# Late expert search spread over five half-table passes, and three-product value matmuls from the middle of the seventh pass

## The chip, the cores and the metric

The kernel runs on one core of one Trainium2 chip. The metric is the device time of one execution in microseconds, lower is better. Times are medians of three runs unless a sentence says otherwise; the profile is one further execution, and all rows come from it.

## What is computed

The reference is one decoder layer on 1024 tokens of width 1024: three gated token mixers, a residual and a LayerNorm, and then a product-key expert layer ("PEER") with a second residual and LayerNorm. The change touches only the expert layer:

```
q  = h @ w_q                                   # 8 heads x 2 halves x 128
s1, i1 = top_k(q1 . keys1, 16);  s2, i2 = top_k(q2 . keys2, 16)
cand = s1[:, None] + s2[None, :]               # 256 candidates of a head
top, pos = top_k(cand, 16);  idx = i1[pos] * 128 + i2[pos]
gate = softmax(top)
act  = gelu(h . u_tab[idx])                    # 128 experts of each token
out  = sum(gate * act * v_tab[idx])
```

`u_tab` and `v_tab` have 16384 rows of 1024 float32 numbers, 64 MB each.

## The kernel before

**Blocks and passes.** The expert layer works on 8 blocks of 128 tokens. The u rows are gathered per token: for one of the 128 slots of a block, POOL issues one indirect DMA that brings 128 rows of 4 KB (512 KB) into one of 7 places of `u_ring` (L994), and DVE multiplies them with the residual and sums (a "dot", L2400). The v rows are not gathered. The 128 token x 128 slot coefficients of a block are spread into a table of 128 x 128 keys (`table`, coefficient of expert row by token, mostly zeros), and the whole value table is streamed past it: SP loads tiles of 128 v rows (512 KB) into the 4 places of `v_ring` (L892), and PE multiplies each tile with the matching column block of `table` and adds into PSUM (`values_of`, L1391). One **pass** streams half of the value table, 64 tiles; a block needs two passes, and two blocks are in flight at a time, so there are nine passes, numbered here 0 to 8 like `p` in the code. Passes 0 and 8 have one block in flight, the others two. A float32 product of 128x512 is two instructions in the profile, so a tile of passes 1 to 6 is 8 of them, a tile of passes 0 and 8 is 4.

**What a pass holds beside the products.** In the first 28 tiles (`DOT_TILES`) of pass p DVE makes the last 56 dots of block p+1, and ACT its GELU, DVE its coefficients (L2405). At tile 30 (`TURN_TILE`) PE transposes keys and coefficients (`turn`, L1070); it waits there for DVE's coefficients. In tiles 32 to 63 the table of block p+1 is built, 4 tokens a tile: DVE makes one-hot rows (`hots`, L2392, L2393), ACT scales them (L1803), PE multiplies them (`pair`, L1377), ACT copies the result into `table` (`pair_out`, L1815). DVE makes the first 72 dots of block p+2 in the same tiles. Only two sets of one-hot buffers exist, so `hots` for one group of tokens waits for the `pair` two groups before.

**The late search.** The experts of blocks 4 to 7 are found while the passes run. Each block has four parts (two heads each); a part is four steps on DVE (`late_topk`), one a tile, and one set of small products on PE (`late_scores`, L1405). `topk_at` places them: passes 0 to 3 each run the four parts of one block in tiles 1 to 23 (a part every `SEARCH_TILES` = 6), at tile 24 the gates of that block (`late_gates`, `late_exps`), and at tile 25 ACT stores picks and gates in DRAM (`late_stored`), from where SP loads them at tile 48 of the next pass (`load_picks`). Most of the search's scratch lies in the one-hot buffers `hot1`, `hot2`, the picks `idxu` too; therefore `hots` waits for the store (`tk_out`).

**The split products.** In pass 7 alone PE runs three fp32r products in place of one float32 product (`split_values_of`, L1423; one instruction each, 12 a tile): coefficient and value are both split into a high part (fp32r) and a low part, and high x high, high x low and low x high are summed. ACT makes the high parts (`high_parts`: two copies of 128x128 from `table`, L1846, then one of the value tile, L1847); DVE subtracts for the low parts (`low_parts`: L2445 twice, then L2447) and so frees the place in `v_ring` (`low_made`, for which SP waits). In every other pass the place is freed by PE (`v_used`). There are two buffer sets: ACT may begin the set of a tile once PE has finished the tile two before (`split_used`). The value parts lie in `u_ring`, which is empty by then, the coefficient parts in `hot1_0` and `hot1_1`.

**The end of a block.** At tile 1 of pass p DVE adds block p-2 from PSUM to the residual (`add_rows`, L2413), after waiting for its last product of the pass before (`closed`); at tiles 3, 4, 7 and 8 it makes the second LayerNorm (`finish`). PE waits for `summed` before it starts the next block in the same PSUM banks.

Of the kernel before, what the change touches and what calls it, by code (L numbers as in the profile page):

```python
# [27 lines left out]
F32 = mybir.dt.float32  # L28
# [41 lines left out]
EARLY_DOTS = 72  # L70
SEARCH_TILES = 6
# [138 lines left out]
def layer(nc, A):  # L210
# [26 lines left out]
    with ctx:  # L237
# [190 lines left out]
        def raw_at(name, offset, k):  # L428
# [9 lines left out]
                    for part in range(2)] for i in range(2)]  # L438
        split_c = [nc.alloc_sbuf_tensor_at(f"split_c{i}", [P, 2, 2, P], F32R, offset=where[f"hot1_{i}"]) for i in range(2)]

        def late_topk_tiles(free):
# [16 lines left out]
            t.idxu = lay("idxu", "hot2_1", 1024, [P, SLOTS], U32)  # L458
# [86 lines left out]
        high_made, low_made, split_used = sem("high_made"), sem("low_made"), sem("split_used")  # L545
# [66 lines left out]
        def last_split(p, i):  # L612

            return NTILE * (p - NBLK + 1) + i
# [59 lines left out]
        def _(sp):  # L674
# [325 lines left out]
        def _(pe):  # L1000
# [397 lines left out]
            def late_scores(p, tb, q):  # L1398
# [3 lines left out]
                if q >= 2:  # L1402
                    pe.wait_ge(TK.sem, TK.after("rest", late_item(tb, q - 2)))
# [4 lines left out]
            def split_values_of(p, i):  # L1408

                m = last_split(p, i)  # L1410
                vhi, vlo = split_v[m % 2]
                c_of = split_c[m % 2]
                for n in in_flight(p):
                    if n == p and i == 0:
                        pe.wait_ge(summed, p - 1)
                    for a, v in ((0, vhi), (0, vlo), (1, vhi)):
                        if n == in_flight(p)[0]:
                            if a == 0 and v is vhi:
                                pe.wait_ge(high_made, m + 1)
                            elif a == 0:  # L1420
                                pe.wait_ge(low_made, m + 1)
                        for c in range(2):
                            last = pe.matmul(ps[2 * (n % 2) + c][:, :], c_of[:, n % 2, a, :], v[:, HALF * c:HALF * c + HALF],  # L1423
# [4 lines left out]
                last.then_inc(split_used, 1)  # L1428
# [7 lines left out]
            for p in range(NBLK + 1):  # L1436
                for i in range(NTILE):
# [18 lines left out]
        def _(act):  # L1456
# [379 lines left out]
            def high_parts(p, i):  # L1836

                j, m = NTILE * p + i, last_split(p, i)
# [16 lines left out]
            for p in range(NBLK + 1):  # L1855
                for i in range(NTILE):
# [4 lines left out]
                    if p == NBLK - 1:  # L1861
                        high_parts(p, i)
                    if p < NB:
                        part = topk_at(p, i)
                        if part and part[2] == 0 and part[:2] != (NB - 1, 3):
                            load_scores(4 * part[0] + part[1] + 1)
                        if i == 4 * SEARCH_TILES:
                            late_exps(p)
                        if i == 4 * SEARCH_TILES + 1:
                            late_stored(p)  # L1870
# [12 lines left out]
        def _(dve):  # L1883
# [139 lines left out]
            def late_topk(tb, q, part):  # L2023
                topk(late, late_item(tb, q), part, 4 + q % 2, late.idxu[:, 2 * TOPK * q:2 * TOPK * (q + 1)], late.gex[:, 2 * q:2 * q + 2, :],
# [351 lines left out]
            def hots(n, sub):  # L2376
# [11 lines left out]
                if sub == 1 and 1 <= n <= NB:  # L2388
                    dve.wait_ge(tk_out, late_stores(n))
# [49 lines left out]
            def low_parts(p, i):  # L2439

                j, m = NTILE * p + i, last_split(p, i)
                dve.wait_ge(high_made, m + 1)
                vhi, vlo = split_v[m % 2]
# [10 lines left out]
            for p in range(NBLK + 1):  # L2454
                for i in range(NTILE):
# [5 lines left out]
                    if p < NB and i == 4 * SEARCH_TILES:  # L2461
                        late_gates(p)
# [5 lines left out]
                    if p == NBLK - 1:  # L2468
# [33 lines left out]
```

## Time and profile before

| | before |
|---|---|
| median of three runs | 4051.45 us (4048.8 to 4055.97) |
| the profiled execution's own time | 4052.45 us |
| its span, first to last instruction | 4050.6 us |
| mean granted TensorE clock | 0.958 of full |
| busy share of the span: PE, DVE, ACT, POOL | 91%, 66%, 31%, 39% |
| bytes moved | 1133.97 MB, mean 280 GB/s |

The span is 1.85 us shorter than the execution's own time, and that execution lies 1.0 us above the median. PE, DVE, ACT and POOL are TensorE (matmul), VectorE, ScalarE and GpSimd; PEld is TensorE's weight load, SP the queue that issues the plain DMAs. The nine passes fill the last 2080 us of the span. A busy PE is not a PE at its peak: a float32 product is counted busy as long as it streams.

### The profile page before, as it was taken

The numbers are of one execution on the slowest core, as the hardware profiler recorded it, in microseconds if no ns is written. First come the engines' busy times: TensorE is split into PE (matmuls) and PEld (weight loads), VectorE is DVE, ScalarE is ACT, GpSimd is POOL, SyncE is SP. The second block draws the span as 40 slices with busy tenths as digits, with TensorE's granted clock in tenths as the row PEclk, the third lists the DMA queues.
The fourth block names the chain that finished last, engine by engine and source line by source line (L and its number), as shares of the span: only waits on it lengthen the run. The fifth ranks groups of instructions, "written<-read, shape, count | busy, mean of one in ns | idle before, by whom it ended". The sixth has DMA issues, their size and how long they took to land.

```text
span 4050.6 us, 45984 instructions
## 1 busy us (share of the span) xinstructions
PE 3694.7 (91%) x14431; PEld 2458.7 (61%) x14431; DVE 2655.6 (66%) x5440; ACT 1235.9 (31%) x2640; POOL 1577.4 (39%) x1341
## 2 busy tenths in 40 slices
PE   6999989898888979867779999898999999999998
PEld 5778768677777768656444454453544545445763
DVE  1445542248777766666999889889877868743540
ACT  1333332222333232224342240330412404224530
POOL 2556534331222157655344443444444444410000
PEclk8999999999999989988889999999999999999999
DMA  7666633346777658878999999999999999963567
GB/s 244 202 226 221 214 101 96 98 154 238 240 222 233 221 183 261 276 237 316 320 379 400 380 394 377 375 378 376 399 401 392 401 410 397 396 256 127 185 204 268
DMA packets 506327, 1133.97 MB, mean 280 GB/s; under 512 B 41180, under 2 KB 250508, under 8 KB 505904
## 3 DMA queue, kind: packets, MB, share of 16 engines
q1 hardware_dynamic: 335120, 570.94, 40.5%
q0 software_dynamic: 147456, 536.94, 35.4%
q10 hardware_dynamic: 23584, 24.12, 1.7%
q8 instruction: 73, 1.20, 0.1%
q14 instruction: 94, 0.77, 0.1%
HBM read 1044.81 MB, written 89.41 MB: 280 GB/s over the span
## 4 chain that ended last, share of the span: by engine, by line
PE 34%; DVE 14%; DMA 3%; issue 2%; ACT 1%; DVEq 0%; ACTq 0%
PE ps L1391 27%; DVE u_ring L2400 5%; PE ps L1377 4%; PE ps L1423 2%; DMA u_ring<-in_peer_u,pidx 2%; DVE split_v L2447 1%; DMA v_ring<-in_peer_v 1%; ACT split_v L1847 1%; DVE hot L2392 1%; DVE hot L2393 1%; DVE inds_own L1961 0%; DVE got_own L2006 0%; DVE inds_own L1949 0%; DVE left_own L1952 0%; ACT split_c L1846 0%
## 5 line engine op out<-in xcount | busy, mean ns | idle before, releaser
L1391 PE MATMUL ps<-v_ring,table 128*128 128x512 f32 x3584 | 1593.0, 595 | 17.4 <-DMA v_ring<-in_peer_v 17.2
L994 POOL DMA_INDIRECT u_ring<-in_peer_u,pidx x800 | 775.1, 969 | 935.6 <-DVE coefe L2400 881.6
L1391 PEld LDWEIGHTS ps<-v_ring,table 128*128 128x128 f32 x3584 | 663.9, 191 | 772.9 <-issue 725.1
L2400 DVE CUSTOM_DVE_ANT_0 u_ring<-u_ring,h_up 128x1024 f32<-128x1024 f32 x800 | 948.2, 1217 | 137.4 <-DMA u_ring<-in_peer_u,pidx 126.5
L1053 PE MATMUL ps<-x_hi,w_hi 128*128 128x512 f32 x1280 | 516.8, 404 | 39.2 <-ACT w_hi L1499 23.6
L1056 PE MATMUL ps<-x_lo,w_hi 128*128 128x512 f32 x1280 | 506.7, 396 | 0.0
L1377 PEld LDWEIGHTS ps<-hot,hot 128*128 128x128 f32 x2048 | 282.2, 203 | 157.0 <-issue 111.1
L938 POOL TENSOR_TENSOR w_lo<-w_raw,w_hi 128x1024 fp32r<-128x1024 f32 x120 | 300.7, 2511 | 197.0 <-ACT w_hi L1499 192.2
L1815 ACT ACTIVATE table<-ps 128x512 f32<-128x512 f32 (+3 forms) x256 | 229.3, 896 | 435.8 <-PE ps L1377 435.8
L1803 ACT ACTIVATE hot<-hot,by_slot 128x128 f32<-128x128 f32 x1024 | 321.2, 388 | 75.7 <-DVE hot L2392 71.0
L959 POOL DMA_INDIRECT e_ring<-in_peer_u,icole x224 | 229.8, 1026 | 274.1 <-DVE dotse L2058 196.2
L1377 PE MATMUL ps<-hot,hot 128*128 128x128 f32 x2048 | 292.1, 289 | 36.7 <-DVE hot L2393 13.7
L1062 PE MATMUL ps<-x_hi,w_lo 128*128 128x512 f32 x1280 | 317.4, 390 | 0.3 <-POOL w_lo L938 0.2
L1053 PEld LDWEIGHTS ps<-x_hi,w_hi 128*128 128x128 f32 x1280 | 246.0, 192 | 94.2 <-issue 13.3
L2392 DVE TENSOR_TENSOR hot<-keys,by_slot 128x512 f32<-128x512 f32 x256 | 177.1, 692 | 183.8 <-PE ps L1377 173.2
L1056 PEld LDWEIGHTS ps<-x_lo,w_hi 128*128 128x128 f32 x1280 | 245.9, 192 | 52.2 <-issue 1.9
L1062 PEld LDWEIGHTS ps<-x_hi,w_lo 128*128 128x128 f32 x1280 | 239.7, 188 | 52.5 <-POOL w_lo L938 2.6
L2058 DVE CUSTOM_DVE_ANT_0 e_ring<-e_ring,h_up 128x1024 f32<-128x1024 f32 x128 | 155.0, 1220 | 127.9 <-DMA e_ring<-in_peer_u,icole 125.0
L946 POOL TENSOR_TENSOR w_hi<-w_raw,zero 128x1024 fp32r<-128x1024 f32 x56 | 110.4, 1972 | 245.1 <-PE ps L1053 112.7
L1423 PE MATMUL ps<-split_v,split_c 128*128 128x512 f32 x768 | 185.6, 397 | 3.6 <-DVE split_v L2447 1.4
L2393 DVE TENSOR_TENSOR hot<-keys,by_slot 128x512 f32<-128x512 f32 x256 | 175.7, 686 | 0.0
L1423 PEld LDWEIGHTS ps<-split_v,split_c 128*128 128x128 f32 x768 | 140.1, 188 | 48.9 <-DVE split_v L2447 18.5
(326 smaller groups left out, 4184.7 us busy)
## 6 DMA issues: line engine op xcount, KB each, us to landing
v_ring<-in_peer_v SPq DMA_DIRECT2D x576, 512.0 KB, 6.8
w_raw<-in_w_in SPq DMA_DIRECT2D x88, 512.0 KB, 5.0
wh_d<-w_hi SPq DMA_DIRECT2D x56, 512.0 KB, 2.6
wl_d<-w_lo SPq DMA_DIRECT2D x56, 512.0 KB, 4.0
w_hi<-wh_d SPq DMA_DIRECT2D x56, 512.0 KB, 4.5
w_lo<-wl_d SPq DMA_DIRECT2D x56, 512.0 KB, 4.7
u_ring<-in_peer_u,pidx POOLq DMA_INDIRECT x800, 9.2
raw_mid<-in_w_branch SPq DMA_DIRECT2D x48, 256.0 KB, 3.3
```

What stands on the lines that cost most here:

```text
L938: pool.tensor_tensor(out=w_lo[b][:, 0:k, :], in0=raw[:, 0:k, :], in1=w_hi[b][:, 0:k, :].bitcast(F32), op=ALU.subtract).then_inc(w_split[b], 1)
L959: pool.indirect_dma_start(out=e_ring[:, s, :], out_offset=None, in_=u_tab, in_offset=bass.IndirectOffsetOnAxis(ap=icole[:, r, s:s + 1], ax ...
L994: pool.indirect_dma_start(out=u_ring[:, slot_of(n, k), :], out_offset=None, in_=u_tab, in_offset=bass.IndirectOffsetOnAxis(ap=pidx[n % 2][ ...
L1053: first = pe.matmul(out, w_hi[b][:, k, :], hi[:, k, :], start=(k == 0), stop=False)
L1056: pe.matmul(out, w_hi[b][:, k, :], lo[:, k, :], start=False, stop=False)
L1062: last = pe.matmul(out, w_lo[b][:, k, :], hi[:, k, :], start=False, stop=(k == k_n - 1))
L1377: last = pe.matmul(build_bank(item)[:, P * m:P * m + P], hot2[sub % 2][:, m, :], hot1[sub % 2][:, m, :], start=True, stop=True)
L1391: last = pe.matmul(ps[2 * (n % 2) + c][:, :], table[:, row_of(n, i1), :], v_ring[:, j % V_TILES, HALF * c:HALF * c + HALF], start=(n == p ...
L1423: last = pe.matmul(ps[2 * (n % 2) + c][:, :], c_of[:, n % 2, a, :], v[:, HALF * c:HALF * c + HALF], start=(n == p and i == 0 and a == 0 an ...
L1803: last = act.activation(hot1[sub % 2][:, m, :], hot1[sub % 2][:, m, :], ACT.Copy, scale=by_slot[:, 2, t0 + m:t0 + m + 1])
L1815: last = act.activation(table[:, r0:r0 + near, t0:t0 + TOK].rearrange("p i t -> p t i"), src[:, :, 0:near], ACT.Copy)
L2400: dve.tensor_tensor_reduce(out=u_ring[:, slot_of(n, k), :], in0=u_ring[:, slot_of(n, k), :], in1=h1_up[:, :, :].rearrange("p c n -> p (c n)"),
```

## The change

Three things are changed, all in the expert layer.

- **Search.** Passes 0 to 3 run three parts each and pass 4 runs four; part number 3p + slot is counted through, so that a block's four parts lie in two passes. Gates and store follow the fourth part of a block by one and two tiles: pass 1 tiles 6 and 7, pass 2 tiles 12 and 13, pass 3 tiles 18 and 19, pass 4 tiles 24 and 25. The picks get a place of their own (`pidx_one`), and `hots` no longer waits for the store.
- **Split products** run from tile 32 of pass 6 to the end of pass 8, in place of pass 7 alone.
- **Three buffer sets** in place of two, the coefficient parts in `score_in` and the last row of `u_ring`. In passes 6 and 7 the high parts of the coefficients move from ACT to DVE, one copy of both blocks (128x256) in place of two; in pass 8 ACT makes the one copy. The low parts of both blocks are one subtraction in place of two. In pass 8, too, `v_ring` is freed by DVE's `low_made` and no longer by PE.

```diff
+SPLITS = 3
...
+        split_c = [nc.alloc_sbuf_tensor_at(f"split_c{i}", [P, 2, 2, P], F32R, offset=o)
+                   for i, o in enumerate((where["score_in"], where["score_in"] + 2 * D, where["u_ring"] + 2 * SPLITS * D * 4))]
...
-            t.idxu = lay("idxu", "hot2_1", 1024, [P, SLOTS], U32)
+            t.idxu = lay("idxu", "pidx_one", 0, [P, SLOTS], U32)
...
+        FIRST_SPLIT = NTILE * (NBLK - 2) + HALF_T
+        def split_at(p, i):
+            return NTILE * p + i - FIRST_SPLIT
+        def rows_at(p, i):
+            rows = sorted(row_of(n, tile_key(p, i)) for n in in_flight(p))
+            return table[:, rows[0]:rows[-1] + 1:max(rows[-1] - rows[0], 1), :]
+        def high_rows(p, i):
+            return (c_last, i + 1) if p == NBLK else (c_made, split_at(p, i) + 1)
...
+        def searched(p):
+            return 3 if p < NB else 4 if p == NB else 0
         def topk_at(p, i):
-            q, step = i // SEARCH_TILES, i % SEARCH_TILES - 2
-            return (p, q, step) if p < NB and q < 4 and -1 <= step < 4 else None
+            slot, step = i // SEARCH_TILES, i % SEARCH_TILES - 2
+            part = 3 * p + slot
+            return (part // 4, part % 4, step) if 0 <= slot < searched(p) and -1 <= step < 4 else None
...
-                old = j - V_TILES - NTILE * (NBLK - 1)
-                if old in range(NTILE):
+                old = j - V_TILES - FIRST_SPLIT
+                if old >= 0:
                     sp.wait_ge(low_made, old + 1)
                 else:
-                    sp.wait_ge(v_used, j + 1 - (NTILE if old >= NTILE else 0))
+                    sp.wait_ge(v_used, j + 1)
...
             def split_values_of(p, i):
...
                             if a == 0 and v is vhi:
+                                pe.wait_ge(*high_rows(p, i))
                                 pe.wait_ge(high_made, m + 1)
...
-                        if p < NB:
-                            pe.wait_ge(TK.sem, TK.after("rest", late_item(p, 3)))
+                        if searched(p):
+                            pe.wait_ge(TK.sem, TK.after("rest", late_item(0, 0) + 3 * p + searched(p) - 1))
...
-                    if p != NBLK - 1:
+                    if split_at(p, i) < 0:
                         values_of(p, i)
                     else:
                         split_values_of(p, i)
...
             def high_parts(p, i):
...
                     act.wait_ge(u_dots, dots_before(NBLK, 0) + U_ROWS)
-                    act.wait_ge(build_out, pair_item(NBLK - 1, NSUB - 1) + 1)
-                if m >= 2:
-                    act.wait_ge(split_used, m - 1)
-                for n in in_flight(p):
-                    act.activation(split_c[m % 2][:, n % 2, 0, :], table[:, row_of(n, tile_key(p, i)), :], ACT.Copy)
-                act.activation(split_v[m % 2][0][:, :], v_ring[:, j % V_TILES, :], ACT.Copy).then_inc(high_made, 1)
+                if m >= SPLITS:
+                    act.wait_ge(split_used, m - SPLITS + 1)
+                if p == NBLK:
+                    act.activation(split_c[m % SPLITS][:, 0:1, 0, :], rows_at(p, i), ACT.Copy).then_inc(c_last, 1)
+                act.activation(split_v[m % SPLITS][0][:, :], v_ring[:, j % V_TILES, :], ACT.Copy).then_inc(high_made, 1)
...
-                if sub == 1 and 1 <= n <= NB:
-                    dve.wait_ge(tk_out, late_stores(n))
...
             def low_parts(p, i):
...
+                if p == NBLK - 1 and i == 0:
+                    dve.wait_ge(build_out, pair_item(NBLK - 1, NSUB - 1) + 1)
+                if p < NBLK:
+                    if m >= SPLITS:
+                        dve.wait_ge(split_used, m - SPLITS + 1)
+                    dve.tensor_copy(c_of[:, :, 0, :], rows_at(p, i)).then_inc(c_made, 1)
                 dve.wait_ge(high_made, m + 1)
-                vhi, vlo = split_v[m % 2]
-                for n in in_flight(p):
-                    dve.tensor_tensor(out=split_c[m % 2][:, n % 2, 1, :], in0=table[:, row_of(n, tile_key(p, i)), :],
-                                      in1=split_c[m % 2][:, n % 2, 0, :].bitcast(F32), op=ALU.subtract)
-                last = dve.tensor_tensor(out=vlo[:, :], in0=v_ring[:, j % V_TILES, :], in1=vhi[:, :].bitcast(F32), op=ALU.subtract)
-                last.then_inc(low_made, 1)
+                dve.wait_ge(*high_rows(p, i))
+                dve.tensor_tensor(out=c_of[:, :, 1, :], in0=rows_at(p, i), in1=c_of[:, :, 0, :].bitcast(F32), op=ALU.subtract)
+                dve.tensor_tensor(out=vlo[:, :], in0=v_ring[:, j % V_TILES, :], in1=vhi[:, :].bitcast(F32), op=ALU.subtract).then_inc(low_made, 1)
...
-                    if p == NBLK - 1:
+                    if split_at(p, i) >= 0:
                         low_parts(p, i)
```

## Rows read from the trace of the kernel before

**Rows 1.** The chain of work that ended last, shares by line (page, part 4).
```profile
PE ps L1391 27%; DVE u_ring L2400 5%; PE ps L1377 4%; PE ps L1423 2%; DMA u_ring<-in_peer_u,pidx 2%; DVE split_v L2447 1%; DMA v_ring<-in_peer_v 1%; ACT split_v L1847 1%; DVE hot L2392 1%; DVE hot L2393 1%; DVE inds_own L1961 0%; DVE got_own L2006 0%; DVE inds_own L1949 0%; DVE left_own L1952 0%; ACT split_c L1846 0%
```

**Rows 2.** Busy time by stretch: halves of passes 0, 3, 4, 6; passes 7 and 8.
```profile
core 0: us, PE busy (x) PEld busy (x) DVE busy (x) ACT busy (x) POOL busy (x), PEclk, DMA share, GB/s
1963.00:2060.00 97.00, 65.82 (x170) 28.34 (x169) 90.23 (x300) 4.95 (x9) 31.19 (x33) 0.89 0.97 357
2060.00:2164.00 104.00, 90.01 (x382) 52.72 (x381) 92.87 (x159) 70.40 (x156) 51.08 (x49) 0.97 1.03 409
...
2701.00:2836.00 135.00, 118.63 (x300) 54.60 (x299) 124.38 (x360) 7.71 (x15) 56.58 (x58) 0.94 0.96 362
...
2974.00:3093.00 119.00, 114.48 (x270) 51.06 (x269) 78.58 (x133) 4.84 (x12) 56.11 (x58) 0.99 1.00 394
...
3600.00:3737.00 137.00, 137.00 (x506) 76.26 (x506) 38.81 (x60) 66.36 (x156) 0.00 (x0) 1.00 0.38 127
3737.00:3926.00 189.00, 185.45 (x770) 140.10 (x769) 110.19 (x203) 93.58 (x192) 0.00 (x0) 1.00 0.57 185
3926.00:4042.00 116.00, 112.67 (x258) 47.46 (x256) 4.61 (x9) 0.20 (x1) 0.00 (x0) 1.00 0.82 283
```

**Rows 3.** Waits at `turn` in passes 0, 1, 2, 3, 4; last, DVE's in pass 4.
```profile
PE ps L1070 <- DVE coefe L2405: 15.3, 1, 15.3
...
PE ps L1070 <- DVE coefe L2405: 3.1, 1, 3.1
...
PE ps L1070 <- DVE coefe L2405: 16.7, 1, 16.7
...
PE ps L1070 <- DVE coefe L2405: 16.4, 1, 16.4
...
PE ps L1070 <- issue: 4.5, 1, 4.5
...
DVE u_ring L2400 <- DMA u_ring<-in_peer_u,pidx: 36.9, 44, 1.4
```

**Rows 4.** Timeline of one tile, second half of pass 6: PE, then ACT, then DVE.
```profile
start us, us, engine line op out<-in xcount [idle before <-releaser]
3659.82 1.05 PE L1377 MATMUL ps<-hot,hot 128*128 128x128 f32 x8
3660.72 3.60 PE L1391 MATMUL ps<-v_ring,table 128*128 128x512 f32 x8
3664.15 1.05 PE L1377 MATMUL ps<-hot,hot 128*128 128x128 f32 x8
...
3660.92 1.07 ACT L1815 ACTIVATE table<-ps 128x512 f32<-128x512 f32 x1 [2.23 <-PE ps L1377]
3661.76 1.25 ACT L1803 ACTIVATE hot<-hot,by_slot 128x128 f32<-128x128 f32 x4
...
3660.92 0.69 DVE L2392 TENSOR_TENSOR hot<-keys,by_slot 128x512 f32<-128x512 f32 x1 [3.03 <-PE ps L1377]
```

**Rows 5.** Timeline of pass 7: ACT, then DVE.
```profile
3800.70 0.51 ACT L1846 ACTIVATE split_c<-table 128x128 fp32r<-128x128 f32 x2 [1.65 <-PE ps L1423]
3801.12 1.04 ACT L1847 ACTIVATE split_v<-v_ring 128x1024 fp32r<-128x1024 f32 x1
3803.44 0.51 ACT L1846 ACTIVATE split_c<-table 128x128 fp32r<-128x128 f32 x2 [1.28 <-PE ps L1423]
...
3806.58 0.51 ACT L1846 ACTIVATE split_c<-table 128x128 fp32r<-128x128 f32 x2 [1.68 <-PE ps L1423]
...
3802.20 0.49 DVE L2445 TENSOR_TENSOR split_c<-table,split_c 128x128 fp32r<-128x128 f32 x2 [1.49 <-ACT split_v L1847]
3802.61 1.22 DVE L2447 TENSOR_TENSOR split_v<-v_ring,split_v 128x1024 fp32r<-128x1024 f32 x1
```

**Rows 6.** The split products by line (min/median/max ns), and PEld's wait for DVE in pass 7.
```profile
L1423 PE MATMUL ps<-split_v,split_c x768: 387/389/793, 3737.3 to 3926.0; 128*128 128x512 f32 x192
...
PEld ps L1423 <- DVE split_v L2447: 18.5, 41, 1.0
```

**Rows 7.** DMA issues of pass 7 and of pass 8: count, KB, median us to landing.
```profile
v_ring<-in_peer_v SPq DMA_DIRECT2D x61, 512.0 KB, 3.4
...
v_ring<-in_peer_v SPq DMA_DIRECT2D x59, 512.0 KB, 4.6
```

More of the change, by code:

```diff
@@ L437, in layer @@
         split_v = [[nc.alloc_sbuf_tensor_at(f"split_v{part}_{i}", [P, D], F32R, offset=where["u_ring"] + (2 * i + part) * D * 4)
-                    for part in range(2)] for i in range(2)]
-        split_c = [nc.alloc_sbuf_tensor_at(f"split_c{i}", [P, 2, 2, P], F32R, offset=where[f"hot1_{i}"]) for i in range(2)]
+                    for part in range(2)] for i in range(SPLITS)]
+        split_c = [nc.alloc_sbuf_tensor_at(f"split_c{i}", [P, 2, 2, P], F32R, offset=o)
+                   for i, o in enumerate((where["score_in"], where["score_in"] + 2 * D, where["u_ring"] + 2 * SPLITS * D * 4))]
+        assert 2 * SPLITS < U_ROWS
         def late_topk_tiles(free):
@@ L634, in dots_by, with gates_at, stores_at @@
             return min(SLOTS, done)
+        def searched(p):
+            return 3 if p < NB else 4 if p == NB else 0
         def topk_at(p, i):
-            q, step = i // SEARCH_TILES, i % SEARCH_TILES - 2
-            return (p, q, step) if p < NB and q < 4 and -1 <= step < 4 else None
+            slot, step = i // SEARCH_TILES, i % SEARCH_TILES - 2
+            part = 3 * p + slot
+            return (part // 4, part % 4, step) if 0 <= slot < searched(p) and -1 <= step < 4 else None
+        def gates_at(p, i):
+            part = topk_at(p, i - 1)
+            return part[0] if part and part[1:] == (3, 3) else None
+        def stores_at(p, i):
+            return gates_at(p, i - 1)
         def head_item(h, c):
@@ L1401, in late_scores @@
                 pe.wait_ge(build_out, pair_item(p, NSUB - 1) + 1)
-                if q >= 2:
-                    pe.wait_ge(TK.sem, TK.after("rest", late_item(tb, q - 2)))
+                if 4 * tb + q >= 3 * p + 2:
+                    pe.wait_ge(TK.sem, TK.after("rest", late_item(tb, q) - 2))
                 for n in range(4):
@@ L1408, in split_values_of @@
             def split_values_of(p, i):
-                m = last_split(p, i)
-                vhi, vlo = split_v[m % 2]
-                c_of = split_c[m % 2]
+                m = split_at(p, i)
+                vhi, vlo = split_v[m % SPLITS]
+                c_of = split_c[m % SPLITS]
                 for n in in_flight(p):
@@ L1422, in split_values_of @@
                         for c in range(2):
-                            last = pe.matmul(ps[2 * (n % 2) + c][:, :], c_of[:, n % 2, a, :], v[:, HALF * c:HALF * c + HALF],
+                            last = pe.matmul(ps[2 * (n % 2) + c][:, :], c_of[:, part_of(n, p, i), a, :], v[:, HALF * c:HALF * c + HALF],
                                              start=(n == p and i == 0 and a == 0 and v is vhi),
@@ L1427, in split_values_of @@
                         last.then_inc(closed, 1)
-                last.then_inc(split_used, 1)
+                if p < NBLK or i < NTILE - 1:
+                    last.then_inc(split_used, 1)
             turn(0)
@@ L1836, in high_parts @@
             def high_parts(p, i):
-                j, m = NTILE * p + i, last_split(p, i)
+                j, m = NTILE * p + i, split_at(p, i)
                 act.wait_ge(v_in[j % V_TILES], 16 * (j // V_TILES) + 16)
@@ L1860, in _ @@
                         root(p - 2)
-                    if p == NBLK - 1:
+                    if split_at(p, i) >= 0:
                         high_parts(p, i)
[L1863 to L1870, printed above, removed]
+                    part = topk_at(p, i)
+                    if part and part[2] == 0 and part[:2] != (NB - 1, 3):
+                        load_scores(4 * part[0] + part[1] + 1)
+                    if gates_at(p, i) is not None:
+                        late_exps(gates_at(p, i))
+                    if stores_at(p, i) is not None:
+                        late_stored(stores_at(p, i))
                     if i == DOT_TILES and p + 1 < NBLK:
@@ L2023, in late_topk @@
             def late_topk(tb, q, part):
+                if tb == 0 and q == 0 and part == 0:
+                    dve.wait_ge(e_out, 32)
                 topk(late, late_item(tb, q), part, 4 + q % 2, late.idxu[:, 2 * TOPK * q:2 * TOPK * (q + 1)], late.gex[:, 2 * q:2 * q + 2, :],
@@ L2460, in _ @@
                         late_topk(*part)
-                    if p < NB and i == 4 * SEARCH_TILES:
-                        late_gates(p)
+                    if gates_at(p, i) is not None:
+                        late_gates(gates_at(p, i))
                     if p >= 2:
@@ L2467, in _ @@
                             finish(p - 2, (3, 4, 7, 8).index(i))
-                    if p == NBLK - 1:
+                    if split_at(p, i) >= 0:
                         low_parts(p, i)
```

11 lines of the change are left out of this document (6 added, 5 removed).

## The prediction

> **What bounds the kernel now.** I read the chain of waits first. Its largest share in the expert layer is PE's value products, then DVE's dots, then the table builds [rows 1]: the end is set by PE, except where DVE makes it wait. The stretches of the passes [rows 2] then show three regimes. In the second half of pass 6 PE is busy 137 of 137 us and DMA moves 127 GB/s: pure PE. In the first half of pass 3 DVE is busy 124.4 of 135 us, in that of pass 4, which has no search, 78.6 of 119 us. In the second half of pass 0 the DMA share is 1.03 at 409 GB/s. The waits say the same from PE's side: at `turn` it waits 15.3, 3.1, 16.7 and 16.4 us in passes 0 to 3 and 4.5 us in pass 4 [rows 3]. Pass 1 hardly waits because more dots of block 2 are made ahead. In pass 4 DVE itself waits 36.9 us for gathered rows [rows 3], so with the search gone the gathers are the next limit. The time-line of a tile gives the prices at the end: a pair build takes 3660.72 - 3659.82 = 0.90 us and a float32 tile 3664.15 - 3660.72 = 3.43 us, 4.33 together [rows 4].
>
> **Search, passes 0 to 3.** One part costs DVE (124.4 - 78.6) / 4 = 11.5 us [rows 2]. In passes 2 and 3 it comes off the wait of 16.7 and 16.4 us, down to some 5 us, which is also what DMA leaves (4.5 in pass 4). PE loses one set of score products too: the two half-passes differ by 16 us, the waits by 11.9 [rows 2, 3], so four sets and the slower clock after a long wait (0.94 against 0.99 [rows 2]) are worth 4 us, one set and most of the clock about 1. I take 12 us for each of these passes. Pass 1 has no wait to lose: 1 us. In pass 0 the part would take 11.5 off 15.3 us, but its first half already moves 357 GB/s with a DMA share of 0.97, and 97 us at 357 GB/s squeezed to the 409 GB/s of the next half is 85 us: at most 12, at least nothing if it is DMA that holds it. I take 10, nearer to the upper end, since DVE, not DMA, is what PE waits for there. Sum: 10 + 1 + 12 + 12 = 35 us gained.
>
> **Search, pass 4.** Four parts on a pass that had none. Its first half becomes that of pass 3 before, 135 for 119 us [rows 2]: 16 us lost. Net of the search: **-19 us**. The gates, the exponentials and the store move to earlier tiles with one answer: ACT is busy under 8 us of these halves [rows 2], and the picks are due at tile 48. The score loads of ACT's queue are as many as before. Dropping the `tk_out` wait in `hots` is worth nothing: two groups of one-hots are made under 7 us of PE work.
>
> **A split tile.** In pass 7 ACT starts a set when PE ends a tile, at 3800.70, 3803.44 and 3806.58: tiles of 2.74 and 3.14 us in turn [rows 5]. The short one is the tile without a wait, 12 products of 0.228 us; every second tile pays 0.4 us because the set comes late: two copies and the value copy 0.42 + 1.04 on ACT, 0.41 + 1.22 on DVE [rows 5], 3.1 us after a tile two before has ended, against 2.74 us. PEld's waits for DVE, 18.5 us in 41 cases [rows 6], are this.
>
> **Second half of pass 6.** 32 tiles go from 4.33 to 2.74 + 0.90 = 3.64 us: 32 x 0.69 = 22 us, less 1 for the first set: **-21 us**. That holds if ACT and DVE make a tile in 3.64. ACT: value copy 1.04, pair copy 0.84 to the next start, four scalings 1.25 [rows 4, 5] = 3.1. DVE: two one-hots of 0.69, the copy of 256 coefficients, their subtraction at 0.49, the value subtraction 1.22. The copy has no row; ACT's two copies are 0.51 and DVE's own two subtractions 0.49, one instruction of 128 numbers is half of that, so 0.25 to 0.51; I take 0.4. Sum 3.5. Both fit, closely; with three sets their hand-overs are off PE's path. What they lose as cover is PE's long float32 tile. POOL has nothing there.
>
> **Pass 7.** Three sets take the wait out: 64 x 2.74 = 175.4, and 1.1 us for the first tiles, where DVE first waits for the table's last copy and then for the last product before `add_rows`: 176.5 for 189 [rows 2]: **-12.5 us**. It can't gain more than that unless a product gets faster than 0.228 us.
>
> **Pass 8.** PE's tile goes from 4 instructions in about 1.72 us (half of 3.43) to 6 x 0.228 = 1.37 us, 88 us for 64. But a place of `v_ring` is now held by ACT and DVE: coefficient copy 0.21, value copy 1.04, subtraction 0.2, value subtraction 1.22 [rows 5], with hand-overs 2.8 us from landing to release. With four places a tile takes (landing time + 2.8) / 4. Landing takes 3.4 us in pass 7 at 185 GB/s and 4.6 us in pass 8 at 283 GB/s [rows 2, 7]: 1.55 us or 1.85 us a tile. I take 1.85, the row of the same rate of loads. That is 118 us; `finish` of block 6 sits between DVE's subtractions and shifts the ring by 3 us. 121 for 116: **+5 us**, bounds -17 and +20 (landing 5.6, if loads delay each other more). The Trainium skill, in "DMA: Bandwidth & Descriptors" under the anatomy of one DMA, puts a transfer at a fixed 2.0 us plus its bytes over 436 GB/s, for 512 KB 3.2 us as an estimate; the lone loads of pass 7 agree (3.4), those of pass 8 don't, and by it a tile would take 1.5 us and the pass about 96 us, which is rival 2.
>
> **The sum.** -19 - 21 - 12.5 + 5 = -47.5 on the profiled execution's 4052.45 us: 4005. It stood 1.0 above the median of the runs; I say **4004 us**.
>
> **Rivals.**
> 1. *The gathers hold the early passes.* The part taken away was hidden: DVE waits for rows in its place, as in pass 4 (36.9 us), and passes 0, 2 and 3 gain a third, 11 of 34 us, while pass 4 still pays. For it: DMA shares of 0.97 to 1.03 [rows 2]. Against: DVE waits on rows only where it has no search. 4004 + 23 = 4027. Chance 0.15.
> 2. *Pass 8 runs at the lone landing time*, 1.55 us a tile: 64 x 1.55 = 99 us for 116, 22 better than forecast: 3982. For it: the ring sends loads farther apart than PE did. Against: DMA's share is 0.82 at 283 GB/s [rows 2], so at 1.55 us (338 GB/s) little is left. Chance 0.14.
> 3. *PE's clock falls in pass 8.* PE would work 1.37 of 1.85 us. The granted clock was 0.89 in the first half of pass 0, where PE was busy 66 of 97 us [rows 2], and a split product then took up to 793 for 389 ns [rows 6]. At half clock all through, a tile takes 2.74 us, 175 us, +54: 4058, no change. Against: pass 0 lost it around one long wait. "TensorE: Matmul & The Clock Gate" in the Trainium skill says that an engine left idle is throttled and activity releases it. Chance 0.05.
> 4. *Slower: ACT and DVE run in lockstep in pass 6.* High parts, low parts, one-hots and scalings each wait for the other engine, with only two one-hot sets. If nothing overlaps, a tile takes 3.1 + 3.5 = 6.6 us: 32 x (6.6 - 4.33) = +73 in place of -21: 4098. It decides from about 5.4 us a tile on (32 x (5.4 - 3.64) = 56 takes up the gain and 8 us more). Against: before, the same one-hot loop left DVE idle 3.03 us a tile [rows 4], and both engines can run a tile ahead. Chance 0.03.
>
> **How the numbers follow.** The forecast has 0.55; the rest, 0.08, are mixtures of its terms' ends, mostly pass 8 slower (landing 5.6: 4019). A measurement of this kernel tells about 0.2%, 8 us, from no change. Forecast, rivals 1 and 2 and nearly all mixtures are faster: 0.93; rival 3, 0.04 same, with 0.01 of it reaching faster by a clock lost only in part; rival 4, 0.03 slower. The range takes in rivals 1 and 2 almost wholly: 3983 to 4027. The forecast alone has 3994 to 4015 (early passes +-7, pass 8 +-8).
>
> **What would show it.** At `turn` waits near 5 us in passes 0, 2, 3 and 16 in pass 4; tiles of 3.64 us in the second half of pass 6, no wait for DVE there; pass 7 about 176 us; in pass 8 PE waiting for `split_v`, loads landing in 4 to 4.6 us, the pass near 120 us. The forecast is wrong if `turn` still waits over 8 us in passes 2 and 3, if pass 6 has PE waiting for ACT or DVE in every tile, or if pass 8 is under 105 or over 135 us.

## The result and the profile after

| | before | after |
|---|---|---|
| median of 12 runs each | 4053.14 us | 4026.95 us |
| lowest and highest | 4042.63, 4060.24 | 4016.5, 4039.03 |
| ratio of the two, 95% interval | | 0.9935 (0.9923 to 0.9946) |
| the profiled execution's own time | 4052.45 us | 4033.38 us |
| from the first product of pass 0 to the last of pass 8 | 2078.9 us | 2048.5 us |

The change makes the kernel 26 us faster, a little over half of the 47 us that were forecast (4004), and the time lies at the upper end of the range of 3983 to 4027. The profiled execution after lies 6.4 us above its median, and its passes start 11 us later than those before (at 1974 for 1963 us), in code that the change doesn't touch. So the two traces are compared by the length of the passes, 30.4 us shorter, and not by their ends.

Busy time of each engine in the halves of the passes after, cut at the first value product of each half (columns as in [rows 2]):

```profile
core 0: us, PE busy (x) PEld busy (x) DVE busy (x) ACT busy (x) POOL busy (x), PEclk, DMA share, GB/s
1974.00:2063.00 89.00, 67.01 (x159) 27.53 (x158) 77.18 (x241) 2.08 (x6) 30.28 (x32) 0.94 0.97 368
...
2426.00:2558.00 132.00, 116.89 (x292) 53.51 (x291) 112.95 (x304) 7.71 (x15) 56.24 (x58) 0.95 0.97 368
...
2696.00:2828.00 132.00, 117.68 (x296) 54.05 (x295) 112.94 (x304) 7.72 (x15) 56.46 (x59) 0.95 0.97 370
...
2966.00:3100.00 134.00, 118.05 (x299) 54.40 (x298) 123.65 (x360) 7.72 (x15) 56.77 (x59) 0.94 0.96 362
...
3611.00:3726.00 115.00, 115.00 (x633) 99.64 (x632) 92.61 (x153) 97.44 (x184) 0.00 (x0) 1.00 0.48 156
3726.00:3901.00 175.00, 174.55 (x769) 143.81 (x768) 124.52 (x203) 69.80 (x69) 0.00 (x0) 1.00 0.62 200
3901.00:4022.00 121.00, 100.54 (x385) 67.47 (x384) 91.97 (x134) 77.97 (x125) 0.00 (x0) 1.00 0.80 267
```

Set beside [rows 2], the last three rows are the split products as forecast: 115 for 137 us, 175 for 189, 121 for 116. The fourth row is pass 4 with its four parts, a copy of pass 3 before. The surprise is the third: pass 3 lost a part, DVE is busy 113 us for 124, yet the half-pass takes 132 us for 135. By the start of each half-pass in the two traces the terms are:

| stretch | before | after | difference | forecast |
|---|---|---|---|---|
| pass 0 | 200.8 | 192.8 | -8.0 | -10 |
| pass 1 | 264.4 | 259.2 | -5.1 | -1 |
| pass 2, first half | 135.4 | 132.6 | -2.9 | -12 |
| pass 3, first half | 135.3 | 131.9 | -3.4 | -12 |
| pass 4, first half | 119.2 | 135.0 | +15.8 | +16 |
| pass 6, first half | 114.1 | 117.1 | +3.1 | 0 |
| pass 6, second half | 137.2 | 115.3 | -21.9 | -21 |
| pass 7 | 189.0 | 175.1 | -13.8 | -12.5 |
| pass 8 | 115.7 | 121.2 | +5.6 | +5 |

The second halves of passes 2 to 5 and pass 5 itself are as they were within 0.3 us. The 3.1 us of pass 6 belong to a longer wait at `turn` (4.2 for 2.8 us) and a dip of the clock after it; it shows in other kernels below too.

Each row of the table is one trace against one trace, and the early passes differ between executions. Over the traces of this and the next section, with the search placed as before and as after the change, pass 0 takes 196.9 to 200.8 us with four parts and 189.5 to 192.8 with three, pass 1 259.8 to 264.4 and 256.8 to 259.4, the first half of pass 2 135.2 to 135.7 and 132.6 to 134.1. The signs hold; the 5.1 us of pass 1 are at the upper end, from middle to middle they are 3.

The waits at `turn` in passes 0, 2, 3 and 4 after, then DVE's wait for gathered rows in pass 3 (what waited, for what, us in total, times, longest):

```profile
PE ps L1099 <- DVE coefe L2434: 4.5, 1, 4.5
...
PE ps L1099 <- DVE coefe L2434: 15.1, 1, 15.1
...
PE ps L1099 <- issue: 14.3, 1, 14.3
...
PE ps L1099 <- issue: 15.9, 1, 15.9
...
DVE u_ring L2429 <- DMA u_ring<-in_peer_u,pidx: 6.9, 9, 1.3
```

In pass 0 the wait fell as forecast, from 15.3 to 4.5 us, but it is not the measure of the gain there: experiments 7 and 8, with the same search, wait 10.9 and 11.1 us at `turn` in a first half that is shorter still (86.4 and 87.0 us for 89.7). PE waits for `v_ring` loads in this half too, 15.3 us after the change and 9.6 and 10.0 in those two. In passes 2 and 3 the wait at `turn` is hardly shorter than before (16.7 and 16.4 in [rows 3]), and a wait of DVE for rows, of which these half-passes had 0.7 us in pass 2 and none in pass 3, stands in the place of the search.

A tile of the second half of pass 6 after, first DVE:

```profile
3660.55 1.22 DVE L2482 TENSOR_TENSOR split_v<-v_ring,split_v 128x1024 fp32r<-128x1024 f32 x1
3661.84 0.69 DVE L2421 TENSOR_TENSOR hot<-keys,by_slot 128x512 f32<-128x512 f32 x1
3662.45 0.68 DVE L2422 TENSOR_TENSOR hot<-keys,by_slot 128x512 f32<-128x512 f32 x1
3663.05 0.28 DVE L2478 CAST split_c<-table 128x256 fp32r<-128x256 f32 x1
3663.85 0.43 DVE L2481 TENSOR_TENSOR split_c<-table,split_c 128x256 fp32r<-128x256 f32 x1 [0.51 <-ACT split_v L1877]
3664.19 1.22 DVE L2482 TENSOR_TENSOR split_v<-v_ring,split_v 128x1024 fp32r<-128x1024 f32 x1
```

The same tile on ACT:

```profile
3661.84 1.12 ACT L1846 ACTIVATE table<-ps 128x512 f32<-128x512 f32 x1 [0.51 <-PE ps L1406]
3662.74 1.07 ACT L1877 ACTIVATE split_v<-v_ring 128x1024 fp32r<-128x1024 f32 x1
3663.72 1.26 ACT L1834 ACTIVATE hot<-hot,by_slot 128x128 f32<-128x128 f32 x4
3665.47 1.13 ACT L1846 ACTIVATE table<-ps 128x512 f32<-128x512 f32 x1 [0.49 <-PE ps L1406]
```

ACT's copies into `table` are 3665.47 - 3661.84 = 3.63 us apart and it idles 0.5 us in each tile, DVE too. PE has no wait there in the trace, so it sets the pace, at the forecast 3.64 us a tile. The coefficient copy on DVE, which had no row before, takes 0.28 us, the low end of its bounds.

### The profile page after: what moved, and what is told of

The parts are those of the page before. It is cut to its first block, busy times and chain, and to the rows that moved or that the text cites. A ratio compares the mean times of both kernels' runs of the same rounds, so it can differ in the third digit from the quotient of the medians.

```text
span 4031.1 us, 47164 instructions
## 1 busy us (share of the span) xinstructions
PE 3658.6 (91%) x14687; PEld 2513.0 (62%) x14687; DVE 2809.6 (70%) x5664; ACT 1322.2 (33%) x2671; POOL 1577.5 (39%) x1341
## 4 chain that ended last, share of the span: by engine, by line
PE 33%; DVE 11%; DMA 6%; issue 2%; ACT 1%; POOL 0%; DVEq 0%; ACTq 0%
PE ps L1420 21%; PE ps L1453 6%; DVE u_ring L2429 5%; PE ps L1406 4%; DMA u_ring<-in_peer_u,pidx 4%; DMA v_ring<-in_peer_v 2%; DVE hot L2421 1%; DVE hot L2422 1%; DVE split_v L2482 1%; DMA score_in<-subkeys_t 0%; DVE got_own L2035 0%; PE h_up L1395 0%; DVE inds_own L1990 0%; DVE inds_own L1978 0%; ACT split_v L1877 0%
## 5 line engine op out<-in xcount | busy, mean ns | idle before, releaser
L1420 PE MATMUL ps<-v_ring,table 128*128 128x512 f32 x3072 | 1367.4, 596 | 19.4 <-DMA v_ring<-in_peer_v 19.2
L1420 PEld LDWEIGHTS ps<-v_ring,table 128*128 128x128 f32 x3072 | 570.1, 192 | 667.8 <-issue 632.4
L1453 PE MATMUL ps<-split_v,split_c 128*128 128x512 f32 x1536 | 370.7, 395 | 20.9 <-DVE split_v L2482 18.8
L1453 PEld LDWEIGHTS ps<-split_v,split_c 128*128 128x128 f32 x1536 | 281.3, 188 | 97.6 <-DVE split_v L2482 35.2
L2421 DVE TENSOR_TENSOR hot<-keys,by_slot 128x512 f32<-128x512 f32 x256 | 176.8, 691 | 96.2 <-PE ps L1406 71.4
L1877 ACT ACTIVATE split_v<-v_ring 128x1024 fp32r<-128x1024 f32 x160 | 168.7, 1057 | 98.1 <-PE ps L1453 98.1
```

Source lines behind the costliest of these rows:

```text
L1420: last = pe.matmul(ps[2 * (n % 2) + c][:, :], table[:, row_of(n, i1), :], v_ring[:, j % V_TILES, HALF * c:HALF * c + HALF], start=(n == p ...
L1453: last = pe.matmul(ps[2 * (n % 2) + c][:, :], c_of[:, part_of(n, p, i), a, :], v[:, HALF * c:HALF * c + HALF], start=(n == p and i == 0 an ...
```

## The experiments

Each time is the median of 4 to 10 runs; the ratio behind it, with its 95% interval, is to the kernel before, run beside it. The lengths of passes come from one profiled execution each.

Two theories stood after the result. **A:** the split products gave all of the gain and the search nothing, because the gathers have no slack: while the parts run DVE is full, the seven places of `u_ring` stay full and the gathers stop; what they miss is not made up. **B:** the bytes of a half-pass bound it, and where the search lies doesn't matter; or the search was worth its forecast and the split fell short.

**1. The split alone.** The search goes back to four parts in passes 0 to 3.

```diff
-            return 3 if p < NB else 4 if p == NB else 0
+            return 4 if p < NB else 0
...
-            part = 3 * p + slot
+            part = 4 * p + slot
```

> The change with the search put back: four parts in each of passes 0 to 3, none in pass 4; the split products and three buffer sets stay. Theory (the moved search gives nothing net; the split products give all of the gain, 21.9 + 13.8 - 5.6 = 30 us by the two traces): 30 us under the kernel before, about 4023 us, with passes 0 to 5 as long as before, the second half of pass 6 at 115 us, pass 7 at 175, pass 8 at 121. Rival (the search was worth its forecast 19 us, and it is the split that fell short): only 7 us under the kernel before.

4026.13 us, 0.9935 (0.9915 to 0.9954) of before: the same as the whole change. The median is 26.5 us under the kernel before where 30 were expected; the passes of the trace are 32.6 us shorter, 7 of them in passes 0 and 1 (197.6 and 260.5 us), whose search is that of before. Its first halves of passes 2 to 4 are 135.2, 135.2 and 118.3 us, as before; pass 6's second half 115.2, pass 7 175.1, pass 8 123.6.

**2. The search alone**, in the kernel before: the parts placed 3, 3, 3, 3, 4, pass 7 alone split, with two sets (the diff is the change's own, without its split parts).

> The kernel before with the search alone moved (3, 3, 3, 3, 4 parts); pass 7 alone is split, with two sets. Theory: within 4 us of the kernel before; the first halves of passes 0 to 3 are shorter by 8, 5, 3 and 3 us, that of pass 4 longer by 16. Rival (the forecast): 19 us faster.

4053.8 us, 1.0002 (0.9993 to 1.0012). The first halves of passes 0 to 4 take 88.7, 117.7, 133.8, 131.9 and 134.7 us: the same pattern as after the whole change. The two runs together settle it: the gain is the split's, and the moved search cancels itself.

**3. and 4. The same parts, placed differently.** In the first the steps of a part lie two tiles apart; in the second the parts follow each other without a free tile. The first `PLACES` below is that of the spread version, the second that of the clumped one.

```diff
-            slot, step = i // SEARCH_TILES, i % SEARCH_TILES - 2
+            per, steps_at = PLACES[searched(p)] if searched(p) else (64, {})
+            slot, step = i // per, steps_at.get(i % per, -2)
...
+PLACES = {3: (9, {1: -1, 2: 0, 4: 1, 6: 2, 8: 3}), 4: (7, {1: -1, 2: 0, 3: 1, 5: 2, 6: 3})}
+PLACES = {3: (5, {0: -1, 1: 0, 2: 1, 3: 2, 4: 3}), 4: (6, {1: -1, 2: 0, 3: 1, 4: 2, 5: 3})}
```

> The change with the same three parts a pass, but their steps two tiles apart over tiles 1 to 26 in place of one tile apart in tiles 1 to 17 (and the four of pass 4 over tiles 1 to 27). Nothing is computed otherwise. Theory (while parts run DVE is full and the gathers stop, because the seven places of u_ring are full; after the last part the dots left over come at the gathers' rate): DVE work of 110 us a first half is then even, the dots never fall behind the gathers, PE's wait at the turn in passes 2 and 3 falls from 15 to 5 or 6 us, each first half from 132 to about 123 us; pass 4 stays at 135 because four parts fill DVE all along; some 20 us under the change, 4007. Rival (the bytes of a first half bound it, DMA share 0.97): placement changes nothing, waits stay at 14 to 15 us, 4027.

> The other direction: the three parts of passes 0 to 3 without a free tile between them, in tiles 0 to 14; pass 4 as in the change. Theory: more dots are left when the parts end (26 for 20 of 58), the wait at the turn in passes 2 and 3 grows from 15 to about 19 us, 10 us over the change in all, 4037. Rival (bytes bound it): no difference.

Spread: 4022.64 us, 0.9923 (0.9901 to 0.9945), first halves of passes 2 and 3 129.6 and 130.9 us, waits 12.6 and 12.7 us. Clumped: 4042.29 us, 0.9977 (0.9965 to 0.9989), 136.4 and 137.9 us, 15 us over the change by the medians where 10 were expected. Its waits at `turn` did not grow to 19 us (14.7 and 14.9): PE itself gets there later, since it waits 3 us near the start, where `add_rows` comes late. Placement matters, so B's bytes alone don't bound it, but spreading brought 1 to 3 us a half-pass where 9 were expected, and by the medians it can't be told from the change. The gathers issued by POOL show why. Windows of 80, 26 and 14 us (20 in the last kernel, the third left out in two of them) from the start of a pass; the columns are POOL's busy time with the number of gathers, the granted TensorE clock, the DMA share and GB/s. First pass 3 after the change:

```profile
2696.00:2776.00 80.00, 30.49 (x31) 1.00 0.98 367
2776.00:2802.00 26.00, 13.58 (x14) 1.00 1.03 412
2802.00:2816.00 14.00, 7.62 (x9) 0.66 1.02 407
```

Pass 3 before, with four parts:

```profile
2701.00:2781.00 80.00, 30.14 (x31) 1.00 0.98 365
2781.00:2807.00 26.00, 11.01 (x12) 1.00 1.03 409
```

Pass 4 before, without a search:

```profile
2974.00:3054.00 80.00, 39.95 (x41) 1.00 1.01 400
3054.00:3080.00 26.00, 11.47 (x13) 1.00 1.03 410
```

Pass 3 with the parts spread:

```profile
2681.00:2761.00 80.00, 37.17 (x38) 1.00 1.00 384
2761.00:2787.00 26.00, 7.51 (x8) 1.00 1.03 409
2787.00:2801.00 14.00, 7.51 (x8) 0.65 1.02 394
```

Pass 3 with the parts clumped:

```profile
2692.00:2772.00 80.00, 28.46 (x29) 0.96 0.91 330
2772.00:2798.00 26.00, 12.17 (x13) 1.00 1.02 405
2798.00:2818.00 20.00, 10.61 (x12) 0.68 1.03 410
```

PE could reach `turn` about 106 us into a pass. By then pass 4 before has issued 54 gathers, pass 3 before 43, the change 45, the spread version 46, the clumped one 42 (a gather on the border of two windows counts in both). In its first 80 us pass 3 after the change runs the same three parts at the same places as before and has the same 31 gathers; leaving out the fourth part gives two gathers more. The rest must come while PE stands (the clock of 0.65 to 0.68 is read over that wait), at 394 to 410 GB/s and some 1.6 us a gather. After the parts DVE waits for rows, so no DVE time can buy the deficit back. The spread version is better early (38 for 31 in 80 us), but its last part runs from 78 to 112 us into the pass, when the change has run its last by 82 us. In pass 3 before, DVE began its coefficients 122.5 us into the pass; the four parts, gates included, kept it busy 12.7 us a part. Three parts leave 122.5 - 12.7 = 110 us of work for 106 us. That is full however they lie. After the change the coefficients began at 119.6 us, some 10 us later than this sum, and DVE stood 9.6 us before its dots that it had not stood before (6.9 for rows, 2.7 with no releaser named). Theory A holds, with its capacity put right: three parts are one too many. A `u_ring` with more places, which would test the gathers' deficit directly, was not run.

**5. Two parts in the late passes.** If so, two parts fit into the 37 us that DVE waits in a pass without search. The rest of the edit is that of 3.

```diff
+PARTS = (4, 4, 4, 2, 2)
+PLACES = {4: (6, {1: -1, 2: 0, 3: 1, 4: 2, 5: 3}), 2: (13, {1: -1, 3: 0, 6: 1, 9: 2, 12: 3})}
```

> The change with the sixteen parts placed 4, 4, 4, 2, 2 on passes 0 to 4; the two parts of passes 3 and 4 have their steps three tiles apart. Theory (from passes 2 and 4 the gathers run at their rate of about 4.8 rows in 10 us and have no slack; DVE work costs nothing while DVE still waits for rows, and costs its full time once DVE is full and the seven places of u_ring stay full): two parts, 25 us, fit into the 37 us that DVE waits for rows, so the first halves of passes 3 and 4 take 119 to 122 us, those of passes 0 to 2 what they took before (97, 122, 135); sum of the five first halves 594 us for 607 of the change, 12 us under the change, 4015. Rival (each part costs a pass about the same, 4 us): 127 us in passes 3 and 4, sum 609, no gain over the change, 4027.

4016.39 us, 0.9905 (0.9887 to 0.9923), by its median 11 us under the change. The first halves of passes 3 and 4 take 122.8 and 121.0 us. The gathers of pass 3, in the same windows:

```profile
2705.00:2785.00 80.00, 38.06 (x39) 1.00 1.02 400
2785.00:2811.00 26.00, 11.40 (x13) 1.00 1.03 410
```

And DVE's wait for rows in it:

```profile
DVE u_ring L2431 <- DMA u_ring<-in_peer_u,pidx: 15.2, 17, 1.5
```

52 gathers by 106 us for 45: two parts come almost free (DVE's wait for rows falls from 36.9 to 15.2 us), and the price of a part is not a constant: against the 119.2 us of pass 4 before, which had none, two parts cost 2 to 4 us a half-pass, three cost 10 to 13 (spread or not), four 16.

**6. Pass 8 in float32.** The split products stop at the end of pass 7.

```diff
-            return NTILE * p + i - FIRST_SPLIT
+            return NTILE * p + i - FIRST_SPLIT if p < NBLK else -1
...
-                if old >= 0:
+                if 0 <= old < NSPLIT:
                     sp.wait_ge(low_made, old + 1)
                 else:
-                    sp.wait_ge(v_used, j + 1)
+                    sp.wait_ge(v_used, j + 1 - (NSPLIT if old >= 0 else 0))
```

> The change with pass 8 alone put back to float32 products, its places in v_ring freed by PE. Theory (the ring of four places bounds pass 8: landing time plus 2.8 us of holding, over four): pass 8 goes back from 121 to 116 us, 5 us under the change, 4022. Rival (pass 8 would be as long with float32 because something else, the loads themselves or the later start of its tiles, sets it): 121 us, no difference.

4014.73 us, 0.9901 (0.9883 to 0.9919). Pass 8 takes 113.6 us for 121.2, PE busy 112:

```profile
3891.00:4005.00 114.00, 112.08 (x260) 48.09 (x258) 4.87 (x9) 0.20 (x1) 0.00 (x0) 1.00 0.83 285
```

So splitting pass 8 costs 7.6 us by the two traces; the medians are 12 apart, with intervals of some 7 us. Over all traces pass 8 takes 113.3 to 115.7 us in the five kernels that have it in float32, and 121.2 to 123.9 in the six that have it split as in the change. Experiment 1's trace shows the ring at work, first the DMA issues of its pass 8 (count, KB, median us to landing):

```profile
v_ring<-in_peer_v SPq DMA_DIRECT2D x59, 512.0 KB, 4.8
```

One tile of that pass on ACT:

```profile
3925.70 0.31 ACT L1876 ACTIVATE split_c<-table 128x128 fp32r<-128x128 f32 x1 [1.07 <-DMA v_ring<-in_peer_v]
3925.92 1.04 ACT L1877 ACTIVATE split_v<-v_ring 128x1024 fp32r<-128x1024 f32 x1
```

And on DVE:

```profile
3927.00 0.29 DVE L2481 TENSOR_TENSOR split_c<-table,split_c 128x128 fp32r<-128x128 f32 x1 [0.75 <-ACT split_v L1877]
3927.20 1.22 DVE L2482 TENSOR_TENSOR split_v<-v_ring,split_v 128x1024 fp32r<-128x1024 f32 x1
```

From ACT's start at 3925.70 to DVE's end at 3928.42 a place is held 2.72 us; with 4.8 us to land, (4.8 + 2.7) / 4 = 1.88 us a tile, and the pass is 123.6 / 64 = 1.93 in that trace and 1.89 after the change. A `v_ring` with more places, which would test the ring directly, was not run. The Trainium skill's fixed time plus bytes for one transfer ("DMA: Bandwidth & Descriptors", anatomy of one DMA; 3.2 us as an estimate) is a fit for transfers that GpSimd issues, and these loads are SP's. It is near the 3.4 us of the lone loads of pass 7 [rows 7]; once loads overlap (4.6 to 4.8 us), the trace does not agree.

**7. Two buffer sets.** `SPLITS = 2`, with the list of places for `split_c` cut to two; nothing else.

> The change with two buffer sets in place of three. Theory (the third set takes out the wait for the low parts): pass 7 back to 187 to 189 us for 175, tiles of 2.74 and 3.1 us in turn; the second half of pass 6, where the pair build of 0.9 us covers the hand-over, within 4 us of 115; pass 8 within 5 us of 121; 13 to 18 us over the change, 4042. Rival (moving the coefficient copies from ACT to DVE took the wait out, not the third set): pass 7 stays near 176 us.

4038.03 us, 0.9966 (0.9951 to 0.9981). The passes from the second half of pass 6 on:

```profile
3592.00:3708.00 116.00, 116.00 (x640) 100.40 (x638) 90.50 (x153) 99.95 (x184) 0.00 (x0) 1.00 0.47 155
3708.00:3885.00 177.00, 176.24 (x767) 143.27 (x767) 122.94 (x201) 69.29 (x67) 0.00 (x0) 1.00 0.60 195
3885.00:4020.00 135.00, 107.04 (x386) 64.98 (x384) 94.81 (x137) 79.41 (x127) 0.00 (x0) 1.00 0.76 243
```

Here the theory falls. Pass 7 takes 177.5 us, hardly more than with three sets, so the third set is not needed to take its waits out. In pass 8, where little was expected, the third set is worth 134.5 - 121.2 = 13 us (11 by the medians): its tiles mostly alternate between 1.66 and 2.40 us with two. Why they do was not followed up.

**8. Three sets, copies back on ACT.**

```diff
-                if p == NBLK:
-                    act.activation(split_c[m % SPLITS][:, 0:1, 0, :], rows_at(p, i), ACT.Copy).then_inc(c_last, 1)
+                for k, n in enumerate(sorted(in_flight(p), key=lambda n: row_of(n, tile_key(p, i)))):
+                    last = act.activation(split_c[m % SPLITS][:, k, 0, :], table[:, row_of(n, tile_key(p, i)), :], ACT.Copy)
+                last.then_inc(c_last, 1)
```

> The change with the coefficients' high parts back on ACT as two copies of 128x128, three sets kept. It tells what took the wait out of pass 7: two sets with the copies on DVE gave 177.5 us, two sets with the copies on ACT (the kernel before) 189, three sets with the copies on DVE 175. Theory (either of the two is enough, since each alone shortens the wait for a set below the 2.72 us of the products): pass 7 at 175 to 178 us, the second half of pass 6 at 115 to 118 (ACT then has 3.6 us of work a tile of 3.63), within 4 us of the change. Rival (only taking the copies off ACT helps): pass 7 at 186 us or more.

4022.38 us, 0.9933 (0.9916 to 0.9949), pass 7 at 175.5, the second half of pass 6 at 115.5 us. With the kernel before (two sets, copies on ACT: 189) the four cases are complete: either step alone takes the wait out (177.5 and 175.5 us), and both together (175.1) add 0.4 to 2.4 us. One thing is not told apart: these three kernels also make the low parts of both blocks in one subtraction, the kernel before in two. By the rows (0.43 us for 0.49, and 0.34 us for 0.41 to the next start) that is worth 0.07 us of the 3.1 that a set took, an estimate; no run has that step alone.

**9. A shorter hold in pass 8.** ACT copies the coefficients before it waits for the value tile, DVE subtracts them before it waits for the high value part.

```diff
-                act.wait_ge(v_in[j % V_TILES], 16 * (j // V_TILES) + 16)
+                if p < NBLK:
+                    act.wait_ge(v_in[j % V_TILES], 16 * (j // V_TILES) + 16)
...
                     act.activation(split_c[m % SPLITS][:, 0:1, 0, :], rows_at(p, i), ACT.Copy).then_inc(c_last, 1)
+                    act.wait_ge(v_in[j % V_TILES], 16 * (j // V_TILES) + 16)
```

> The change with pass 8's coefficient parts made before the value tile has landed: ACT copies them before it waits for the tile, DVE subtracts them before it waits for the high value part. Theory (ring): a place is held 0.4 us less, a tile takes 0.1 us less, pass 8 about 115 us for 121, 6 us under the change, 4021. Rival (DVE or the loads' rate bounds pass 8): at most 1 us.

4020.34 us, 0.991 (0.9887 to 0.9933), by the medians not clear of the change. Pass 8 takes 119.1 us, 2.1 less than after the change and not 6; it lies below all six split traces above, by 2.1 to 4.8 us. The time-lines of SP, ACT and DVE give both terms of the ring, as means over pass 8. From ACT's first use of a place to its release: 2.81 us after the change, 2.41 here, the 0.4 us that were meant. From the issue of a load to that first use: 4.83 and 5.15 us, 0.3 more. The ring holds as a sum, (5.15 + 2.41) / 4 = 1.89 us a tile, but its two terms are not independent. Part of the 0.3 us is in the loads: in tiles where ACT stood waiting for its load the time from the issue is 4.74 and 5.00 us. That the loads queue on each other because they are issued closer together is argued, not shown.

**10. and 11. Put together.** The first takes 5 and 6. The second places the parts 3, 4, 4, 3, 2, the threes spread.

> The change with both gains of the single experiments: the parts placed 4, 4, 4, 2, 2 and pass 8 in float32 products. Theory (they are in different passes and add): 12 + 7.5 us under the change, 4007 us. Rival (one took what the other gave, or the single ones were noise): 4015, as either alone.

> As the run before, but the parts placed 3, 4, 4, 3, 2, those of passes with three parts spread two tiles apart. Theory: the first half of pass 0 at 86 to 90 us for 95 to 97, that of pass 3 at 130 for 123, the rest the same; within 3 us of the run before, 4006. Rival (a lead won in pass 0 is lost in pass 1, which waits for the same gathers): 5 us slower than the run before.

4006.46 us, 0.9895 (0.9878 to 0.9911), and 4003.26 us, 0.9883 (0.9866 to 0.9899). The two gains add. Either version beats both kernels, by 20 to 24 us the change and by 45 to 48 the kernel before; the two can't be told apart (pass 0's first half is 84.2 us for 98.0, pass 3's 130.2 for 122.9). In the first one the sum of the passes is 2022.0 us for 2048.5 after the change, in the second 2026.9. The lead that pass 0 wins is not lost in pass 1 (259.7 and 259.8 us), against the last rival.

## Why the prediction was right and wrong

The direction and the three terms of the end were right, each within 2 us by the trace: **pass 6** -21.9 for -21, **pass 7** -13.8 for -12.5, **pass 8** +5.6 for +5. **Pass 4** (+15.8 for +16) was right because pass 3 before was its exact model. **Pass 0** gave 8 of 10.

The step that failed is "In passes 2 and 3 it comes off the wait of 16.7 and 16.4 us, down to some 5 us". The wait stayed at 15.1 and 14.3 us, over the 8 that the prediction itself named as the sign of being wrong, and the half-passes gave 2.9 and 3.4 us in place of 12 each, 17.7 us short. The search as a whole came to -3.6 us for -19, since pass 1 gave 4 us more than forecast. The 11.5 us of DVE time did go (busy 124.4 to 112.9 us). The step in effect took the time to the coefficients for the larger of two times, DVE's 110 us of work and the 107 us at which the gathers let pass 4 have them without a search. But the two share a buffer of seven rows: in a time when DVE is full the gathers lose what they can't catch up, since once DVE frees places DMA already moves 394 to 412 GB/s. So the times partly add. The rows for it stood in the prediction, DVE's 36.9 us of waiting for rows in pass 4 above all, and rival 1 named the mechanism, with a third of the gain left (4027). In passes 2 and 3 it was this rival that came true, at 3 of 12 us. What was argued against it, that DVE waits on rows only where it has no search, is true of the first halves before (to within 2 us) only because there DVE was the longer of the two. That the median, 4026.95 us, falls on rival 1's figure is partly luck: rival 1 gave passes 0, 2 and 3 together 11 us and they took 14, pass 1 took 4 more than forecast, pass 6 lost 3 in its first half, and the two traces differ by 30.4 us where the medians differ by 26.2.

Pass 1 was missed the other way, -5.1 for -1 (some -3 over all traces): its wait at `turn` of 3.1 us, taken as a floor, vanished, and so did a set of score products.

In pass 7 the size was right and the cause half right. "Three sets take the wait out" was one of two sufficient causes; experiments 7 and 8 show that moving the copies does it as well. In pass 8 the ring of four places gave the right time, 1.85 us a tile and 3 us for `finish` (1.89 measured over the pass, both together). That the third set matters most there, 13 us, the prediction did not see.

Rival 2 (lone landing times) fell: loads took 4.8 us in experiment 1's pass 8. Rival 3 fell: the granted clock was 1.00 over pass 8 with PE busy 100.5 of 121 us. One of its rows was misread as well: the product of 793 ns is the first of pass 7, at 3737.3 us, in 10 us with a granted clock of 1.00; pass 0 has no split products, and the row shows nothing of the clock. Rival 4 fell: 3.63 us a tile, both helpers idle 0.5 us of it.

## What to carry to other kernels

A wait that names one engine is worth its length only if the next resource has room; where a second resource, coupled to it through a short ring, is within a few per cent of the limit, its time adds to the first one's in part. Work that fits into the first engine's idle waits is nearly free, the next piece is not. Place such work by count per stage (here two parts, not three), and test by placement, which changes no work. Before a product is made cheaper, check how long the cheaper form holds its input's buffer: in pass 8 PE's work on a tile went from about 1.72 to 1.37 us, and the tile from 1.78 (experiment 6) to 1.89.

## What was not expected of the hardware

- A DMA share of 0.96 to 0.98 did not mean full: the first halves of passes 0, 2, 3 and 4 with three or four parts of the search showed it at 357 to 370 GB/s, the other half-passes up to pass 5 had 1.00 to 1.03 at 384 to 409 GB/s. Here the bytes moved told of headroom, the share hardly did.
- Split products of 128x512, each with a weight load before it, start 0.228 us apart before the change and 0.227 after (medians over pass 7), though after it DVE has ended a tile's low parts 2.5 us before PE starts the tile.
- The front part of the kernel, unchanged in all of these, ended between 1962 and 1974 us; a difference under 10 us between two single executions has to be looked for in the passes.
